# A transformer block with routed experts and a second block on one core: norms, transposes, router and rank handed on in smaller pieces

## The reference, cut to what matters

```python
h = rms_norm(x, attn_norm)
x = x + hybrid_mixer(h, ...)      # h @ w_in; 8 forget-gate heads and 8 sliding-window heads;
                                  # merged = g_f * (o_f @ w_proj_fox) + g_s * (o_s @ w_proj_swa); merged @ w_out
h = rms_norm(x, ffn_norm)
x = x + hier_moe(h, ...)          # 64 experts in 8 groups: best group by softmax, best 2 experts in it
x = rms_norm(x, final_norm)
# second block
xn = rmsnorm(x, pre_mix_norm)
x = x + rmsnorm(token_mixer(xn), post_mix_norm)      # retention (4 heads) and latent attention (8 heads), w_o
hn = rmsnorm(x, pre_ffn_norm)
x = x + rmsnorm((silu(hn @ w_gate) * (hn @ w_up)) @ w_down, post_ffn_norm)
x = x + rmsnorm(p @ w_ple_proj, ple_norm) * sigmoid(x @ w_ple_gate + b)
```

## Time and profile before

| what | value |
|---|---|
| median of 3 runs | 2256.28 us (2253.89 to 2257.93) |
| the profiled execution | 2254.45 us, span 2252.7 us |
| PE busy | 1871.4 us, 83% of the span |
| VectorE busy | 798.6 us, 35% |
| ScalarE busy | 694.0 us, 31% |
| POOL busy | 40.8 us, 2% |
| read from HBM | 498.03 MB, 222 GB/s over the span |

### The profile page before, as it was taken

The page is one execution under the profiler, slowest core; times in us unless marked ns, Lnnn a source line. Parts: engine busy times, 40 slices in busy tenths (PEclk is TensorE's granted clock), DMA queues, the critical chain, the costliest instruction groups (busy, mean ns, idle before and its releaser), DMA issues.

```text
span 2252.7 us, 35882 instructions
## 1 busy us (share of the span) xinstructions
PE 1871.4 (83%) x14468; PEld 1266.2 (56%) x14468; DVE 798.6 (35%) x1526; ACT 694.0 (31%) x1266; POOL 40.8 (2%) x150
## 2 busy tenths in 40 slices
PE   6998998767777777777777777499889799998988
PEld 4775787644343443343443343268456688887876
DVE  4436325342222222222222222742465423332245
ACT  3337422222222222222222222322335422221142
POOL 0000000000000000000000000200000000000000
PEclk9999999979999999999999999799899899999999
DMA  5230121559999999999999999122110223233220
GB/s 155 85 117 15 51 99 56 201 217 426 426 426 427 427 426 426 425 427 428 425 427 426 425 427 415 55 88 65 43 44 29 60 90 104 83 112 112 94 75 38
DMA packets 109572, 501.11 MB, mean 222 GB/s; under 512 B 12856, under 2 KB 60216, under 8 KB 76480
## 3 DMA queue, kind: packets, MB, share of 16 engines
q1 hardware_dynamic: 102880, 491.01, 54.7%
q10 hardware_dynamic: 5952, 7.04, 1.0%
q0 software_dynamic: 672, 2.11, 0.3%
HBM read 498.03 MB, written 2.11 MB: 222 GB/s over the span
## 4 chain that ended last, share of the span: by engine, by line
PE 57%; DMA 27%; DVE 8%; ACT 4%; issue 2%; SPq 1%; ACTq 0%; DVEq 0%; POOLq 0%; POOL 0%
DMA ring<-in_w 26%; PE bank L562 12%; PE bank L563 12%; PE bank L564 12%; PE bank L1855 7%; PE bank L1827 3%; PE bank L1846 3%; DVE w_lo L640 2%; ACT w_hi L631 1%; DMA raw<-in_w_in 1%; PE bank L704 1%; PE bank L557 1%; PE bank L728 1%; PE bank L716 1%; SPq L1528 1%
## 5 line engine op out<-in xcount | busy, mean ns | idle before, releaser
L1855 PE MATMUL bank<-ring,XTs 128*32 128x256 f32 x4096 | 288.9, 430 | 112.1 <-DMA ring<-in_w 111.4
L640 DVE TENSOR_TENSOR w_lo<-raw,w_hi 128x2048 fp32r<-128x2048 f32 (+3 forms) x84 | 184.4, 2196 | 443.9 <-ACT w_hi L631 443.7
L2046 DVE TENSOR_TENSOR x<-x,bank 128x512 f32<-128x512 f32 x264 | 163.9, 682 | 488.5 <-PE bank L1846 488.5
L562 PE MATMUL bank<-hTh,w_hi 128*128 128x512 f32 (+1 forms) x728 | 290.9, 400 | 15.8 <-DVE w_lo L640 12.9
L1855 PEld LDWEIGHTS bank<-ring,XTs 128*32 128x32 f32 x4096 | 143.1, 121 | 259.6 <-issue 201.8
L563 PE MATMUL bank<-hTh,w_lo 128*128 128x512 f32 (+1 forms) x728 | 287.9, 395 | 0.0
L564 PE MATMUL bank<-hTl,w_hi 128*128 128x512 f32 (+1 forms) x728 | 285.4, 392 | 0.0
L631 ACT ACTIVATE w_hi<-raw 128x2048 fp32r<-128x2048 f32 (+3 forms) x84 | 153.8, 1832 | 247.5 <-PE bank L564 239.4
L1864 PE MATMUL bank<-ring,aT 128*32 128x256 f32 x2048 | 123.8, 382 | 89.0 <-DVE aT L2066 89.0
L562 PEld LDWEIGHTS bank<-hTh,w_hi 128*128 128x128 f32 (+1 forms) x728 | 137.1, 188 | 56.6 <-DVE w_lo L640 19.3
L1693 ACT ACTIVATE y<-bank 32x256 f32<-32x256 f32 x256 | 96.1, 376 | 220.7 <-PE bank L1846 136.8
(11 more groups left out here) (356 smaller groups left out, 2258.6 us busy)
## 6 DMA issues: line engine op xcount, KB each, us to landing
ring<-in_w SPq DMA_DIRECT2D x192, 2048.0 KB, 19.6
raw<-in_w_in SPq DMA_DIRECT2D x24, 1024.0 KB, 5.4
raw<-in_w_gate SPq DMA_DIRECT2D x11, 1024.0 KB, 5.3
raw<-in_w_up SPq DMA_DIRECT2D x11, 1024.0 KB, 5.3
raw<-in_w_down SPq DMA_DIRECT2D x11, 1024.0 KB, 4.9
raw<-in_w_out SPq DMA_DIRECT2D x4, 1024.0 KB, 5.0
raw<-in_w_o SPq DMA_DIRECT2D x4, 1024.0 KB, 5.2
raw<-in_w_ple_gate SPq DMA_DIRECT2D x4, 1024.0 KB, 5.0
```

The lines of the kernel that those rows point to most:

```text
L562: pe.matmul(dst, left[0], right[0], start=start, stop=False)
L640: v.tensor_tensor(w_lo[:, k % PARTS, 0:size], raw[:, k % RAW, 0:size], w_hi[:, k % PARTS, 0:size].bitcast(F32), ALU.subtract).then_inc(lo_ ...
L1855: mm = pe.matmul(Hb[BLK * j:BLK * (j + 1), :], XTs[u][:, 4 * (c % 2) + 2 * h + c // 2, :], w[:, at_:at_ + Q], start=(h == 0 and c == 0), s ...
L2046: ins = v.tensor_tensor(xs, xs, Sb[t % 2][n][:, :], ALU.add)
```

## The change

- **Norms per tile.** Norms n1 and n2 use a new class `TileNorm`: square, mean, root and reciprocal of one tile, then the next tile. `pe_to_feature` can wait tile by tile; it then runs tiles outside and chunks inside, and all banks fill during the last tile (hT1, hT3, hT4, hT5).
- **Start.** `qs` runs ahead of `zT`, reading each chunk as it is split.
- **Out projection.** The low half of `merged` chunk c-1 follows the addition of chunk c, and PE waits for four chunks ahead of the first unit of out0, for eight ahead of the second (and again, fulfilled, in out1).
- **Router stage.** Each tile is normed between the additions of out1, transposed into two banks (`rows_turned`), evacuated (`turned`), and its router follows the next tile's transposes.
- **Rank.** `both`, the triangle and the ones are bf16, the counts stay exact; rank, count, starts and further get fixed banks.
- **First expert.** VectorE forms `oh[0]` right after `r_over`, PE gathers between the matmuls of `starts` and `further`, evacuations and transposes follow ahead of `m_ready`; the gates' arithmetic moves behind `r_further`. POOL waits for `tab` instead of `m_ready`. The ring buffer of expert 1's third matrix is loaded after `ps`.
- **End of the experts.** The two splits of ScalarE go behind the loop, the angles of rope2 into the last pair, those of rope3 into two parts between the splits for rq and rk; the squares of n3 and n4 are taken in turn; the split of VectorE goes behind the flushes; POOL's product waits for `xn4`; the positions are loaded ahead of the loop.
- **Down.** The first unit of `down` is split during the last gate and up job.

```diff
-        def pe_to_feature(pe, jobs, src, nt=NT):
-            for c, job in enumerate(jobs):
+        def pe_to_feature(pe, jobs, src, ready=None):
...
+            for job in jobs:
                 claim(pe, job)
-                for i in range(nt):
+            for i in range(NT):
+                ready(i)
+                for c, job in enumerate(jobs):
                     mm = pe.transpose(banks[job.bank][:, P * i:P * (i + 1)], src(i, c), ident)
-                fill(mm, job)
+                    if i == NT - 1:
+                        fill(mm, job)
+
+        class TileNorm:
+            def __init__(self, name):
+                self.squares, self.means, self.roots = S(name + "_squares"), S(name + "_means"), S(name + "_roots")
+
+            def act(self, act, i, src, junk, into, r):
+                act.activation(junk, src, ACT.Square, accum_out=into[:, i:i + 1]).then_inc(self.squares, 1)
+                act.wait_ge(self.means, i + 1)
+                act.activation(r[:, i:i + 1], r[:, i:i + 1], ACT.Sqrt).then_inc(self.roots, 1)
+
+            def dve(self, v, chain, i, ss, r):
+                v.wait_ge(self.squares, i + 1)
+                v.tensor_scalar(r[:, i:i + 1], ss[:, i:i + 1], 1.0 / D, EPS, ALU.mult, ALU.add).then_inc(self.means, 1)
+                v.wait_ge(self.roots, i + 1)
+                chain(v.reciprocal(r[:, i:i + 1], r[:, i:i + 1]))
@@ PE, start
-            pe.wait_ge(S("xn1"), NT)
-            pe_to_feature(pe, J["hT1"], lambda i, c: xn(i)[:, P * c:P * (c + 1)])
-
+            pe_to_feature(pe, J["hT1"], lambda i, c: xn(i)[:, P * c:P * (c + 1)], lambda i: pe.wait_ge(S("xn1"), i + 1))
+
+            pe_feature(pe, "qs", hT, fresh="hT1")
             pe.wait_ge(S("wf_lo"), 1)
...
-            pe_feature(pe, "qs", hT)
             read(pe, J["zT"])
@@ PE, out projection and router
-            pe.wait_ge(S("merged_lo"), DC)
             for n in range(2):
-                pe_token(pe, f"out{n}", hT)
+                pe_token(pe, f"out{n}", hT, wait=lambda k: pe.wait_ge(S("merged_lo"), 4 * (k + 1)))
...
+            for i in range(NT):
+                rows_turned(i)
+                if i:
+                    router(i - 1)
+            router(NT - 1)
@@ PE, first expert
+            pe.wait_ge(made_oh, 1)
+            gather(0)
+
             job = J["further"][0]
             claim(pe, job)
             pe.wait_ge(S("r_further"), 1)
...
-            pe.wait_ge(made_oh, 1)
-            gather(0)
             pe.wait_ge(xe_out, 1)
             rows_to_columns()
+            for job in J["before_moe"]:
+                if job.bank:
+                    claim(pe, job)
+            pe.wait_ge(m_ready, 1)
+            count = pe.value_load(blk[0:1, NX:NX + 1], min_val=NE // 2 - 1, max_val=NBLK // 2 - 1)
@@ SP
-            full(sp, order[n_first - 1].last)
...
-            for u in range(2):
-                for m in range(3):
-                    load_matrix(u, m, u)
+            full(sp, J["ps"][-1])
+            load_matrix(1, 2, 1)
+            full(sp, order[n_first - 1].last)
+            for u, m in ((0, 0), (0, 1), (0, 2), (1, 0), (1, 1)):
+                load_matrix(u, m, u)
@@ VectorE, merged and norm n2
+                if c:
+                    merged_lo(c - 1)
+            lo_until(v, units_of["out0"][0].n)
+            merged_lo(DC - 1)
...
+            def rows_normed(i):
+                if i >= 0:
+                    n2.dve(v, chain, i, ssq, rstd)
+                    if i == 0:
+                        v.wait_ge(S("w_r"), 96)
+                    v.scalar_tensor_tensor(h2[:, i, :].rearrange("q (c p) -> q c p", c=DC), by_eighths(x[:, i, :]),
+                                           rstd[:, i:i + 1], by_eighths(row_gain), ALU.mult, ALU.mult).then_inc(S("h2"), 1)
+                if i >= 1:
+                    turned(i - 1)
@@ VectorE, last pair
+                    if last:
+                        if u == 0:
+                            v.wait_ge(S("w_pos2"), 16)
+                            chain(v.tensor_copy(k2, pos2.bitcast(I32)))
+                            chain(v.tensor_copy(pos2, k2))
+                        dve_angles(v, chain, "rope2", C("inv_ret"), cos2, sin2, pos2, ang2, k2, (u,))
@@ ScalarE, end of the experts
-                    if u and last:
-                        hi_at.limit = len(order)
-                        hi_until(act, n_first + 1)
...
+            chain(act.activation(rstd2[:, 0:1], ssq[:, 0:1], ACT.Sqrt))
+            hi_at.limit = len(order)
+            hi_until(act, n_first + 1)
@@ second block, VectorE
-            v.wait_ge(S("w_pos2"), 16)
-            chain(v.tensor_copy(k2, pos2.bitcast(I32)))
-            chain(v.tensor_copy(pos2, k2))
-            dve_angles(v, chain, "rope2", C("inv_ret"), cos2, sin2, pos2, ang2, k2)
-            dve_angles(v, chain, "rope3", C("inv_mla"), cos3, sin3, pos2, ang3, k3)
-            for name in ("rq", "rk"):
+            for part, name in enumerate(("rq", "rk")):
                 ahead(lo_until, v, name, len(J[name]) - 1)
+                dve_angles(v, chain, "rope3", C("inv_mla"), cos3, sin3, pos2, ang3, k3, (part,))
@@ second block, down
+                if f == FC - 1:
+                    lo_until(v, units_of["down"][0].n)
```

239 lines of the change are left out of this document (136 added, 103 removed).

## The result

The changed kernel takes 2196.01 us (median of 4 runs, 2195.99 to 2196.90), the one before 2255.09 (4 runs beside it, 2253.45 to 2257.93): ratio 0.9738, 95% interval 0.9721 to 0.9755, 59.1 us less. The forecast was 2194 with a range from 2184 to 2213. The profiled execution took 2196.03 us, span 2194.2.

What follows compares the result with a forecast made beforehand. The loop was taken as bound by gapless expert-weight transfers from the first buffer release, PE as the bound outside it. Terms 4.0 + 8.1 + 9.5 + 8.4 + 25.4 - 1.5 + 8.9 - 0.8 = 62.0 gave 2194 us, range 2184 to 2213.

Steps and rivals of the forecast that it cites:

- Start, 4.0: Start: PE's first product comes at 23.4 instead of 28.30 us, less 0.8 for `zT`; net 4.0 us, bounds 0 and 5.
- the last `xn` is no earlier: Start: with norms tile by tile, the last `xn` was reckoned at 18.5 us both before and after.
- Out projection, 8.1: Ahead of `out0`: PE's 6.32 us wait and 1.8 us at the lower clock go; 8.1 us, bounds 6.3 and 8.4.
- Norm, transposes, router, 9.5: From `out1` to the last logits: VectorE paces at 4.4 us a tile, logits at 440.3; 9.5 us, bounds 5 and 11.
- Choice to `hidden`, 8.4: Expert choice to `hidden(0, 0)`: 2.6 us from bf16 and 5.8 from work done before the table; bounds 3.5 and 9.5.
- The clock rival: Router stage and expert choice: PE's clock falls in the new gaps and the loop starts late; 2203 us, chance 0.14.
- End of the experts, 25.4: Last pair to `rq`/`rk`: waits of 23.0 us and 2.4 us of lower clock go; 25.4 us, bounds 20 and 27.
- The term for POOL's multiply: End of the experts: with the multiply waiting, `xn4` takes 2.7 us, not 4.4, and small operations no longer lose a microsecond.
- the rival at 0.10: Inside `rq`/`rk`: the 12.61 us stall is not gone but comes one unit later, behind `rope3`; 2207 us, chance 0.10.
- Second block: After the experts' end: `hT4` loses 1.5 us, `down` gains 8.9 as its wait goes, `hT5` loses 0.8.
- the rival by which it loses pace (2287): Expert loop: PE releases buffers late in every pair, 3 us a pair giving 2287 us; chance 0.03.
- the signs by which the prediction would have been wrong: Transfers not gapless once begun, PE waiting over 2 us behind `m_ready`, or angles holding up more than one copy.

Runs made afterwards that it cites:

- the undone order: Changed kernel with `zT` ahead of `qs` again, the norms staying tile by tile: 2200.24 us, 4.2 more than the changed kernel.
- the experiment's median: Changed kernel with the low halves of `merged` made after the last chunk again and PE waiting for all eight ahead of `out0`: 2203.76 us, 7.8 more.
- u_pool: Changed kernel with POOL's multiply released by `xg` again instead of by the last `xn4`: 2197.64 us, 1.6 more.
- p_angles: Changed kernel with the 18 steps of rope2's angles spread over VectorE's gaps in the last pair: 2191.59 us, 4.4 less.
- u_rank: Changed kernel with `both`, the triangle and the ones in f32 again for rank and count: 2199.51 us, 3.5 more.
- u_gather: Changed kernel with PE's gather of expert 0 and the two transposes behind it moved back behind `m_ready`: 2198.01 us, 2.0 more.
- the experiment -0.3: Changed kernel with transposes `hT4` and `hT5` waiting for all four tiles and running chunk by chunk again: 2192.48 us, 3.5 less.

## Why the prediction was right, point by point

The forecast, -62.0 against a measured -59.1, and its main reading held: the loop takes its 912 us from the first release, wherever that lies. Its sum is right to 3 us partly because errors cancel, so the terms matter more.

- **Start, 4.0.** Measured 4.5, over ten traces 4.4 to 5.9; by the undone order 4.2, or 4.4 by its trace. The step "the last `xn` is no earlier" failed by a microsecond, as a tile needs no table load of its own; that microsecond changes nothing, because the splits were the bound.
- **Out projection, 8.1.** Measured 8.1 in the difference of the traces, 7.8 by the experiment's median and 8.6 by its trace.
- **Norm, transposes, router, 9.5.** Measured 10.9. The pace of 4.4 us a tile was reckoned for VectorE; the four `h2` stand 3.6, 3.9 and 3.2 us apart (408.49, 412.11, 416.03, 419.24). Square and root of a tile run beside VectorE's other work, so that the round trip of 1.0 us is not paid in full, and the last tile has no addition left ahead of it. The clock stayed at 1.00.
- **Choice to `hidden`, 8.4.** Measured 6.0 up to the first release. The path to `hidden(0, 0)` came as forecast: from the last logits to its start there were 26.47 us before and are 17.92 now, 8.6 less. From `both` ready to the start of `hidden` it is 10.8 us by the sum (9.8 and 1.0) and 10.8 by the trace (433.16 to 443.95). That this fits so well is luck, as two sizes were off against each other. bf16 brought 4.2, not 2.6 and above its bound of 4; all the rest brought some 4.3 and not 5.8, 0.5 of it because the entry took 1.5, not 1.0. The step that failed is what lies behind: I had taken the first expert as costing what it cost before, and named its lower clock only in the lower bound and in the rival. It ran at the lower clock, 3.64 us instead of 1.93, and the gather behind it took 2.89 instead of 1.94. The clock rival thus came true for 2 to 3 us and not for the router part. Before the change the gather ended 1.6 us ahead of `hidden(0, 0)`, and the clock was back at 1.00. Now the gather comes before the table, and PE waits 3.61 us ahead of `hidden(0, 0)`. In seven of the ten traces with this order and without extra products the clock had come back to 1.00 and fell again in this wait; in `u_pool`, `p_angles` and `u_rank` it had not come back at all. The wait is not the whole cause: in `u_gather` it is 0.67 us and the first expert takes 3.49. The Trainium skill ("TensorE: Matmul & The Clock Gate", HAM oscillation) describes short bursts of products between waits, each of which starts cold; the trace agrees for the waits of 7.31 and 3.61 us ahead of the counts and the first expert. The gaps of 0.4 to 1.0 us between the transposes of the router stage are much shorter, and the clock there is 1.00.
- **End of the experts, 25.4.** Measured 23.2. The shortfall lies mostly ahead of `rq`: counted from the first raw load, its first product gained 8.4 (49.45 before, 41.05 now), where the sum has it at 1434.8 instead of 1444.96, 10.2. The wait for `Hs` was forecast at 3.2 and is 3.8. Not in the sum was that `down` behind it runs cold (3.50 against 1.93, 1.6 lost), and a new wait of 1.0 us for the rotation at 1459.52. The eight splits beside POOL lost nothing, as I took; the low half of the second weight unit lost 0.9 (3.15 against 2.28), and PE did not wait for it. The term for POOL's multiply was oversized: `xn4` gained what I said, but PE's transposes would have hidden about 1 us of it. That the stall of `rq` is gone and not moved was the rival at 0.10, and is excluded.
- **Second block.** `down` 8.9 forecast, 8.5 measured. `hT4` -1.5 forecast; the difference of the traces leaves -0.8 and the experiment -0.3. Here I costed the later first bank in full, but the old order had PE's own 32 transposes in the way, so that the products start equally long after `xn6` (7.6 and 7.7 us). `hT5` -0.8 forecast, -1.5 measured, of which the lower clock behind an idle PE is the part that I named but priced too low.

The loop gave back 0.4 us, and the rival by which it loses pace (2287) has nothing for it. Of the signs by which the prediction would have been wrong none came: from the table (442.46) to `hidden` are 1.5 us, below the 2 that it named.

## What to carry to other kernels

Where a stream of loads is gapless from its first release on, find that release and treat everything ahead of it as if it were on the critical path, one to one; then check the claim by moving the release, not the loads. When work is moved into a busy stage, list the gaps of its engine there and cut the work to their size: the same 18 instructions cost 5 us as two blocks and nothing measurable as four pieces. And a producer that starts earlier is no gain by itself: price what PE's clock does in the wait that it opens behind it.
